# Third attention of a two-block transformer kernel: query turn behind the first scores, compressed groups between the branches, six masks on TensorE, output product begun in thirds

## What is computed

```python
z = h @ w_in                                   # q: 16 heads x 64; three key/value sets; 3 gates a head
k_cmp = silu(blocks(k) @ w1[0]) @ w2[0]        # 15 compressed keys and values of 32 positions each
v_cmp = silu(blocks(v) @ w1[1]) @ w2[1]
p_c = masked_softmax(q @ k_cmp.T * scale, cmp_end <= t);  o_c = p_c @ v_cmp
# n_sel = min(8, 4): with 256 positions all four blocks of 64 are selected,
o_s = masked_softmax(q @ k_s.T * scale, causal) @ v_s     # so this branch is causal attention
o_w = masked_softmax(q @ k_w.T * scale, causal) @ v_w     # the window of 512 is wider than 256
y = (g0 * o_c + g1 * o_s + g2 * o_w) @ w_out
```

## Time and profile before

| | us |
|---|---|
| median of 3 runs | 1501.52 (1500.71 to 1504.72) |
| the profiled execution | 1505.73 |
| its span | 1504.0 |
| TensorE matmul busy | 1451.7 (97%) |
| VectorE busy | 1053.3 (70%) |
| ScalarE busy | 730.8 (49%) |
| GpSimd busy | 77.3 (5%) |

### The profile page before, as it was taken

How to read it: one execution, slowest core, us unless ns; L and a number is a source line. 1 busy time by engine, 2 the same in 40 slices (tenths; PEclk the granted TensorE clock), 3 DMA queues, 4 the chain that set the end, 5 groups by cost and what they waited for, 6 DMA issues and landing times.

```text
span 1504.0 us, 18769 instructions
## 1 busy us (share of the span) xinstructions
PE 1451.7 (97%) x7206; PEld 1196.0 (80%) x7206; DVE 1053.3 (70%) x1428; ACT 730.8 (49%) x1108; POOL 77.3 (5%) x133
## 2 busy tenths in 40 slices
PE   8998999999999999999999999999999888999998
PEld 7886877888877888888778888788888767788886
DVE  4787565887777777766677777877777679685554
ACT  6546545444455434365554343544345665544342
POOL 7200000000000000010100000000000000000000
PEclk9999999999999999999999999999999999999999
DMA  8851434697856978634568787598783600576560
GB/s 286 297 184 41 168 112 168 233 323 253 276 177 225 329 247 279 235 119 141 177 230 295 264 283 267 187 310 272 262 298 116 219 17 1 182 252 212 181 209 28
DMA packets 189087, 314.21 MB, mean 209 GB/s; under 512 B 6896, under 2 KB 100440, under 8 KB 189000
## 3 DMA queue, kind: packets, MB, share of 16 engines
q1 hardware_dynamic: 148800, 232.87, 46.5%
q10 hardware_dynamic: 38408, 75.65, 14.1%
q0 software_dynamic: 1792, 4.51, 0.9%
HBM read 311.92 MB, written 1.07 MB: 208 GB/s over the span
## 4 chain that ended last, share of the span: by engine, by line
PE 84%; DVE 8%; ACT 4%; issue 2%; DMA 1%; POOL 0%; ACTq 0%; POOLq 0%; DVEq 0%
PE ps L1194 25%; PE ps L1196 24%; PE ps L1195 24%; PE ps L1203 5%; PE ps L1526 2%; PE ps L1341 2%; PE ps L1472 1%; DVE wlo L1150 1%; DVE rmax L2369 1%; DVE tmp L2053 1%; ACT whi L1131 1%; DMA raw<-in_nsa_w_out 0%; ACT sp L1894 0%; DVE wide L1150 0%; ACT pT L1902 0%
## 5 line engine op out<-in xcount | busy, mean ns | idle before, releaser
L1150 DVE TENSOR_TENSOR wlo<-raw,whi 128x2048 fp32r<-128x2048 f32 (+2 forms) x168 | 381.4, 2273 | 112.1 <-ACT whi L1131 111.7
L1194 PE MATMUL ps<-whi,aT 128*128 128x512 f32 (+3 forms) x1000 | 399.7, 400 | 6.0 <-DVE aTl L2041 4.0
L1196 PE MATMUL ps<-wlo,aT 128*128 128x512 f32 (+3 forms) x1000 | 388.2, 388 | 0.0
L1195 PE MATMUL ps<-whi,aTl 128*128 128x512 f32 (+3 forms) x1000 | 387.1, 387 | 0.0
L1131 ACT ACTIVATE whi<-raw 128x2048 fp32r<-128x2048 f32 (+2 forms) x166 | 314.0, 1895 | 31.2 <-PE ps L1196 24.2
L1194 PEld LDWEIGHTS ps<-whi,aT 128*128 128x128 f32 x1000 | 188.5, 189 | 49.1 <-issue 9.2
L1196 PEld LDWEIGHTS ps<-wlo,aT 128*128 128x128 f32 x1000 | 188.0, 188 | 39.5
L1195 PEld LDWEIGHTS ps<-whi,aTl 128*128 128x128 f32 x1000 | 188.7, 189 | 34.1
L1836 ACT ACTIVATE hT<-ps 128x256 fp32r<-128x256 f32 (+1 forms) x102 | 42.2, 414 | 343.4 <-PE ps L1203 343.4
L1194 PE MATMUL ps<-whi,hT 128*128 128x512 f32 (+1 forms) x364 | 141.3, 390 | 1.4 <-ACT z L1811 1.4
L1196 PE MATMUL ps<-wlo,hT 128*128 128x512 f32 (+1 forms) x364 | 138.4, 382 | 0.0
(11 more groups left out here) (271 smaller groups left out, 2037.9 us busy)
## 6 DMA issues: line engine op xcount, KB each, us to landing
raw<-in_ff_w SPq DMA_DIRECT2D x176, 512.0 KB, 4.9
raw<-in_ff_w SPq DMA_DIRECT2D x44, 1024.0 KB, 5.3
qT<-in_ada_w ACTq DMA_DIRECT2D x36, 1024.0 KB, 6.6
pT<-in_ada_w ACTq DMA_DIRECT2D x36, 1024.0 KB, 7.1
raw<-in_w_up SPq DMA_DIRECT2D x16, 1024.0 KB, 6.1
raw<-in_w_down SPq DMA_DIRECT2D x16, 1024.0 KB, 5.7
raw<-in_w_in SPq DMA_DIRECT2D x9, 1024.0 KB, 8.8
raw<-in_w_ckv SPq DMA_DIRECT2D x8, 1024.0 KB, 5.1
```

The source lines that it names most:

```text
L1150: dve.tensor_tensor(lo_of(u), raw_of(u), hi_of(u).bitcast(F32), ALU.subtract).then_inc(w_lo, 1)
L1194: pe.matmul(out_ap, hi, w, start=start, stop=False)
L1195: pe.matmul(out_ap, lo, w, start=False, stop=False)
L1196: return pe.matmul(out_ap, hi, wl, start=False, stop=stop)
```

## The change

- `cmp_turn`: the two copies to `hidc` move from VectorE to ScalarE, which then does one Exp of a single element (its function table is loaded there).
- `cmp_out` is no longer behind the last unit of the input product. It is split: its key part runs at step 2 of the attention, ahead of the gate, its value part at step 5. The first compressed scores (now group 8) wait for both.
- The turn of the last eight heads' queries moves to step 0 of the attention, behind the scores of groups 0 and 1, with both copies on VectorE; the scores of group 2 wait for them.
- The four compressed groups come between the branches.
- Six groups of tile 1 (branch 0 with heads 0 and 4, branch 1 all four) get `psum`.
- The finish: step 20 the turn of the first four chunks and the first out product for tile 0; step 21 the same for tile 1, behind the values of group 19; step 22 the turn of the last four chunks, one round a row tile, and the second product.

```diff
             def turn_hid():
-                r = p.rounds(2, "D")
+                r = p.rounds(2, "A")
                 p.stage("cmp_turn", rounds=r, hid=list(r_cmp))
+                r_cmp[:] = r
                 p.turned("q_nsa", 2, ["A", "D"], c0=0)
                 turned.extend(p.keys_turned)
-                r_cmp[:] = r
-            def cmp_out():
-                r = p.rounds(2, "D")
-                p.stage("cmp_out", rounds=r, turned=list(r_cmp))
-                p.turned("q_nsa", 2, ["A", "D"], c0=512)
-                turned.extend(r + p.keys_turned)
+            late = {8: []}
+            def cmp_out(kv):
+                r = p.rounds(1, "D")
+                p.stage("cmp_out", kv=kv, rounds=r, turned=list(r_cmp))
+                late[8] += r
+            def cmp_out_then_gate():
+                cmp_out(0)
+                p.gate(layer, 5)
+            def turn_q_rest():
+                p.turned("q_nsa", 2, "D", c0=512)
+                late[2] = p.keys_turned
...
-                     inner={2: keys, 3: rows, 5: hidden, 6: turn_hid, 7: cmp_out})
+                     inner={2: keys, 3: rows, 5: hidden, 6: turn_hid})
             def finish():
                 p.o_turn(0, "nsa", 10)
-                early(0)()
+                early(0, 0)()
             def finish_rest():
-                p.o_turn(4, "nsa", 12)
+                p.o_turn_tiles(4, "nsa", 12)
                 early(1)()
-            attend("nsa", turned, A["nsa_w_out_2"][0], (p.n_gates + 1, 1.0), {2: lambda: p.gate(layer, 5), 21: finish, 22: finish_rest})
+            attend("nsa", turned, A["nsa_w_out_2"][0], (p.n_gates + 1, 1.0), {0: turn_q_rest, 2: cmp_out_then_gate, 5: lambda: cmp_out(1), 20: finish, 21: early(0, 1), 22: finish_rest}, late=late)
...
         for br in (0, 1):
+            if br:
+                spec += [dict(kind="cmp", t=t, h0=h, nh=8) for h in (0, 8) for t in range(NT)]
             spec += [dict(kind="nsa", br=br, t=t, h0=h, nh=4) for t in range(NT) for h in (0, 4, 8, 12)]
-        spec += [dict(kind="cmp", t=t, h0=h, nh=8) for h in (0, 8) for t in range(NT)]
...
-        g["psum"] = g["kind"] in ("swa", "diff", "mla", "cross")
+        g["psum"] = g["kind"] in ("swa", "diff", "mla", "cross") or g["kind"] == "nsa" and g["t"] == 1 and (g["br"] + (g["h0"] < 8) > 0)
...
-                                                 start=True, stop=kind == "nsa")
+                                                 start=True, stop=not g["psum"])
...
-                                elif kind != "nsa":
+                                elif g["psum"]:
                                     last = masked(sv[:, 2 * i:2 * i + 2, nk - P:nk], causal_r[:, :])
...
+            def cmp_turn(st):
+                for kv, t in enumerate(st["rounds"]):
+                    act.wait_ge(t_ready, t + 1)
+                    act.activation(hidc[:, kv, :], tbank(t)[:, 0:32], ACT.Copy).then_inc(t_act, 1)
+                act.activation(dsk[:, 0, 1, 0:1], dsk[:, 0, 0, 0:1], ACT.Exp)
...
-            def cmp_turn(st):
-                for kv, t in enumerate(st["rounds"]):
-                    dve.wait_ge(t_ready, t + 1)
-                    dve.tensor_copy(hidc[:, kv, :], tbank(t)[:, 0:32]).then_inc(t_dve, 1)
```

More of the change, by code:

```diff
@@ L1591, in cmp_out @@
             def cmp_out(st):
-                for kv, t in enumerate(st["rounds"]):
+                kv = st["kv"]
+                for t in st["rounds"]:
                     wait_emptied(pe, T, lambda j: st["turned"][kv])
@@ L1963, in _ @@
                          q_mla=turns_of, k_mla=turns_of, q_nsa=turns_of, k_nsa=turns_of, w_nsa=turns_of, o_T=o_T,
-                         attend=attend, attend_head=attend, conv=conv, cmp_rows=cmp_rows, cmp_hid=cmp_hid,
+                         attend=attend, attend_head=attend, conv=conv, cmp_rows=cmp_rows, cmp_hid=cmp_hid, cmp_turn=cmp_turn,
                          out_first=out_first, out_rest=out_rest)
@@ L2587, in _ @@
                          out_rest=out_rest, cmp_rows=cmp_rows, cmp_hid=cmp_hid,
-                         cmp_turn=cmp_turn, cmp_out=cmp_out, mla_pack=mla_pack)
+                         cmp_out=cmp_out, mla_pack=mla_pack)
             for st in p.stages:
```

## The result

The changed kernel takes **1511.89 us** (median; 1510.72 to 1513.69) beside 1502.06 us for the kernel before on the same chip (1500.71 to 1504.72): ratio 1.006, 95% interval 1.0039 to 1.0081. It is slower by 9.8 us, where the forecast had 2.3 us less, 1499.2 us, in a range that ended at 1504.0. Run again unaltered (`e9_after_again`), it took 1511.38 us, ratio 1.005 (1.0034 to 1.0065).

A forecast was written before the change was run, and what follows sets the result against it. TensorE's queue was taken to bound the kernel (84% of the chain). Terms -3.3 - 5.8 + 1.1 + 5.6 gave -2.4, unrounded -2.3 us, so 1501.5 - 2.3 = 1499.2 us, range 1494.0 to 1504.0.

The forecast's parts named there:

- Step 1: Compressed hidden rows copied by ScalarE: TensorE's wait falls from 2.0 to 0.4 us, 1.6 us slow clock goes; -3.3 us.
- Step 2: Scores right behind the product: 10.1 us to the scores of group 4 instead of 15.9; -5.8 us.
- Step 3: Masks on TensorE for six groups: 1.5 us more for TensorE, 7.3 us less for VectorE; net left to the layout.
- Step 4: Compressed products inside the attention: TensorE waits 2.6 us for group 5's values; 15.2 against 14.1 us, +1.1 us.
- Step 5: Compressed groups between the branches, finish in thirds: VectorE sets the pace for eight groups; +5.6 us.
- VectorE over 95% busy between the branches: Sign named for the compressed groups between the branches, where VectorE was to set the pace.
- (b): One slow stretch after the 2.6 us wait, 3.4 us at half speed costing 1.7; 1500.9 us, chance 0.28.
- (d): Clock low for long at the head, group 5's values and last compressed turns; +7.4 us, 1508.9 us, chance 0.09.
- (a): The forecast itself: the layout holds, with no clock drop that binds; 1499.2 us, chance 0.35.
- (c): TensorE, not VectorE, sets the pace and waits of 2.6 and 2.0 us vanish; -6.9 us, 1494.6 us, chance 0.25.
- (e): ScalarE reaches the hidden rows no sooner, its split waiting for a weight transfer; +1.0 us, 1502.5 us, chance 0.03.
- The two rules: ScalarE's table load: 1.28 us, no drain, price near zero in the new order; TensorE's clock: lower level followed long waits.

The follow-up runs named there:

- e9_after_again: The changed kernel run again unaltered, against the kernel before; 1511.38 us, ratio 1.005.
- e10: Kernel before plus eleven throwaway 128x128 products in its 2.8 us wait before the first probabilities are turned; 1501.61 us, ratio 0.9989.
- e2: Changed kernel without the six masks on TensorE, VectorE adding them as before; 1513.45 us, ratio 1.0072.
- e6: Changed kernel without the six masks on TensorE, plus ten throwaway products in the wait before group 5's values; 1508.72 us, ratio 1.0034.
- e1: Changed kernel plus ten throwaway 128x128 products inside the wait before group 5's values; 1501.96 us, ratio 0.9996.
- e3: Changed kernel with the compressed groups back at the end, all else as changed; 1502.10 us, ratio 0.9998.
- e7: Changed kernel plus ten throwaway products issued behind the wait for group 5's copies, which stays empty; 1506.22 us, ratio 1.0023.
- e4_step1: Kernel before with only the hidden-row copies and the early Exp on ScalarE; 1499.77 us, ratio 0.9984.

## Why the prediction was wrong

**The queues were right.**
- Step 1, forecast -3.3. From the start of the wait on the hidden rows to the product's end: 1201.38 - 1191.35 = 10.0 us before, 1197.00 - 1190.31 = 6.7 after. Right against the trace that it was read from, and the wait is 0.32 where 0.4 was forecast. But it is too much for the kernel: in the trace of `e10`, whose instructions are the same up to there, the wait is 0.69 and the same distance 1199.18 - 1192.11 = 7.1, so that in such an execution step 1 gains 0.4.
- Step 2, 10.1 us from the product's end to the scores of group 4: 1207.17 - 1197.00 = 10.2. Right, with waits of 1.28, 1.23 and 0.64 for 1.4, 1.5 and 0.6.
- Step 3: VectorE lost 7.6 us, 7.3 of additions and 0.3 of copies that ScalarE has now. The masks net 2.1 us in the changed kernel (`e2` against both runs of it) for 1.9 in the layout, though with unequal slow stretches (20.5 and 23.9 us); at equal clocks `e6` less `e1` gives 2.6. Right in the main.
- Step 4, 15.2 us to the first compressed scores: 1223.80 - 1207.17 = 16.6. The 1.4 more is the first slow stretch of this stage (1206.9 to 1210.3, at 0.54): the scores and masks of group 4 take 3.4 us from start to start, those of group 5 (1211.82 to 1213.77 in the same timeline) 1.95. Both traces of the changed kernel have this stretch; in that of `e1`, the same kernel up to there, it is missing and the distance is 1224.10 - 1208.88 = 15.2. VectorE's idling (over 3 us; 3.25) and the wait of TensorE (2.6; 2.40) are as forecast.
- Step 5, 5.6 us more than before (its terms as written, 11.7 - 6.9 + 1.0, add up to 5.8). Before, from the scores of group 8 at 1231.39 to the start of the second output product below, it is 55.9 us, so 61.5 were forecast. The changed kernel has 70.4. With the wait filled it is 61.6. "VectorE over 95% busy between the branches" did not come: 50% in the slow stretch, 84% with the clock held.

```profile
1287.30 0.48 PE L1194 MATMUL ps<-whi,aT 128*128 128x512 f32 x1
```

**The step that failed is the clock behind the new wait of 2.6 us.** The sum has it at nothing ("no drop that binds"). The text named the mechanism as a rival: (b) put one slow stretch at this very wait, (d) put long ones at three places and gave that 0.09. Both took the length from stretches of the kernel before, and so a price of 1.7 and 3.4 us at this place, half of 3.4 and of 6.8 us. It was 23.9 us long and cost 8.9. The forecast asked how long the wait is and not what TensorE does behind it. (b) even had the clue, "TensorE is dense there for 8 us", and took 3.4 us from another place all the same. TensorE was busy 23.90 of 23.90 us here, and the clock was back only at 1251.2. That the stretch is over after 6.8 us when other work stands behind the same wait is shown (`e3`, `e7`), by one trace each and by their times; what in that work does so is not, since size, number and kind of the products change together.

**A second error was in the sum.** Of the forecast's gain, 4.5 us was slow clock taken away (1.6 in step 1, 2.9 in step 2), read from one execution, 4.2 us above the median, and then taken in full from the median. Not every execution has it to give back: in the trace of `e10` the stretch behind the hidden rows, and most of the wait ahead of it, are missing, and step 1 alone gained 1.6 us beside the table load where 3.3 were booked. With the clock held in the new order the gain is 0.7 us, not told from none, instead of 2.3; and at equal clocks the new order is 2.0 us slower than the old. The change was forecast faster only because the clock was to be better, and the layout that said so made a new wait of 2.6 us.

**The error in numbers:** forecast -2.3, measured +9.8 against the same chip's kernel before. The stretch behind the wait of group 5 is 9.4 of the 12.1 between them (1511.4, both runs of the changed kernel, against 1502.0 filled). What the kernel with the wait filled lacks of the forecast gain, 2.3 - 0.7 = 1.6, is the next part, and the relief counted in full is the likely reason. The last 1.1 is spread between runs: the changed kernel was 1511.9 in four executions and 1511.4 in ten, the kernel before 1502.06 in four and 1502.7 in all.

**The rivals.** (a), 1499.2, is 2.8 us below `e1_fill`'s 1502.0, where the clock was held; that is inside the range. (c), that TensorE sets the pace, fell: with the clock held, TensorE still has five waits of 0.84 to 1.84 us between the compressed groups and the finish. (d) had sign, mechanism and place, at under a third of the length. That its 1508.9 is near the 1511.9 measured is in part luck: it is the sum of three places, and nearly all came from one. (e) fell: ScalarE was 2.20 us idle before its copies, waiting for TensorE.

**The two rules.** The table load: in `e4_step1` taking it out of the chain shortened the wait by 1.28 us, its own duration, and the first exponential started straight behind it. The drain of the Trainium skill's price (ScalarE: Activation LUTs, What ACT_TABLE_LOAD costs), about 2.7 us in all, is not in these traces. The clock: executions of the kernel before spread from 1498.7 to 1508.8 us at clocks of 0.989 to 0.998, so its drops do come and go. Ten executions of the changed kernel lie at 0.986 to 0.989, and its two traces show the same stretch within 0.2 us. The Trainium skill (TensorE: Matmul & The Clock Gate, What's actually happening) says that the gate runs free of the kernel's start, so that the number of slow matmuls at the start of one kernel differs from run to run. That a drop in the middle may come or not is what the forecast made of it; the first of these findings agrees with that, the second does not. The forecast gave a drop, (b) and (d) together, 0.37.

## What to carry to other kernels

Lay out the queues at full clock and keep slow clock in a column of its own: what a slow stretch costs belongs to the execution it was read from, not to the edit that happens to remove its wait. The same holds for a wait: the one on the hidden rows was 2.04 us in one trace and 0.69 in another, with the same instructions ahead of it, so read a second trace before booking what its removal saves. For each wait that a new order puts on TensorE, as long as those which the trace shows ahead of the lower level, look at what TensorE does next: behind 2.4 us of waiting, values, turns and 30-column scores ran at half speed for 18.7 us and the first wider products for 5.2 more; with wider scores or 128x128 products sooner it was 3.4 to 6.8 in all. If such a wait can't be scheduled away, try throwaway products that fit into it; here ten of them, 2.5 us of work, saved 9.4 us. Eleven in the 2.8 us wait of the old order brought 1.2 us, not told from none.

## What the runs showed of the hardware

- A stretch at 1.2 GHz can outlast the wait ahead of it tenfold: 23.9 us (changed kernel, two traces) and 20.5 us (`e2`) behind 2.40 us, with TensorE busy throughout.
- The same ten 128x128 products kept the clock at 1.00 when they lay inside the wait (`e1`); when they stood behind it, the clock fell, and rose again after 6.8 us (`e7`).
- Several waits of about a microsecond with little between them can be followed by a drop as one long one was: 0.6, 1.1 and 1.1 us ahead of 1204.1 in `e10`, and four of about 1.0 us, 3.9 to 4.7 us apart, ahead of 1275.9 in `e6`. It is not sure: the same 0.6, 1.1 and 1.1 us in the traces of before and of `e4` were followed by full pace (twelve records in 3.08 us).
- A median hides this: `e6` ran at 1501.8 and at 1511.0 us with the same instructions, and its granted clock (0.998 and 0.989) told which.
